# An encoder block on 8 cores: the last FFN product in one pass over 22 tiles, the attention accumulator kept by residue class, V and ones as column halves, x loads ahead of the constants

## What is computed

```
h = rms_norm(x, norm1_g)
proj = h @ w_in                                  # (2048, 9728)
# dilated: 3 groups, (window, dilation) = (128,1), (512,4), (2048,16), 8 heads of 64
#   per group: o_g = softmax(q k^T/8 - slope*dist, banded) v ; lse_g = m + log(denom)
#   merged over groups with softmax(lse) = sum_g numer_g / sum_g denom_g
x = x + (gates0*(y_dil@w_bd) + gates1*(y_ret@w_br) + gates2*(y_mem@w_bm)) @ w_out
u, gate = split(rms_norm(x, norm2_g) @ w_ffn_in)  # 2 x 2816 = 2 x 22 tiles of 128
x = x + (gelu(conv3(u) + b) * gate) @ w_ffn_out
```

## Time and profile before

| | us |
|---|---|
| median of 3 runs | 5742.73 (5291.3 to 5944.16) |
| profiled execution | 5273.2 |
| span of its slowest core (core 6) | 5271.6 |
| spans of the 8 cores | 5244.9 to 5271.6 |
| mean granted TensorE clock, by core | 0.988 to 0.991 |

### The profile page before, as it was taken

One profiled execution on the slowest core, in us unless ns is written; L12 is line 12 of the kernel. 1 busy time (PEld: TensorE's weight loads), 2 busy tenths in 40 slices (PEclk: granted clock), 3 DMA queues, 4 the chain that ended last, 5 costly groups with the idle time before them and its releaser, 6 DMA issues.

```text
span 5271.6 us, 85660 instructions; the slowest of 8 cores (5244.9 to 5271.6 us)
## 1 busy us (share of the span) xinstructions
PE 5008.7 (95%) x29335; PEld 2683.7 (51%) x29816; DVE 3290.3 (62%) x4398; ACT 2393.5 (45%) x4180; POOL 830.4 (16%) x874
## 2 busy tenths in 40 slices
PE   6999999999999999999999999999999999999999
PEld 3556644444455664444455666444445566544444
DVE  5566676656556667664656666766465666776544
ACT  5756543313376664331337665432134756633211
POOL 1322212111222110200112111020021211102000
PEclk9999999999999999999999999999999999999999
DMA  8368797766613335524350434542453143444344
GB/s 161 58 109 136 129 209 201 135 144 146 192 31 87 105 99 184 170 68 134 120 170 22 106 99 119 168 158 72 132 158 120 39 106 99 141 152 140 95 138 120
DMA packets 655785, 655.18 MB, mean 124 GB/s; under 512 B 368128, under 2 KB 411776, under 8 KB 655360
## 3 DMA queue, kind: packets, MB, share of 16 engines
q1 hardware_dynamic: 517712, 607.04, 39.6%
q0 software_dynamic: 137648, 42.64, 8.2%
HBM read 429.46 MB, written 212.34 MB: 122 GB/s over the span
## 4 chain that ended last, share of the span: by engine, by line
PE 85%; DMA 5%; DVE 4%; issue 3%; ACT 2%; POOL 1%; SPq 1%; DVEq 0%; ACTq 0%; POOLq 0%; another core or an unknown queue 0%
PE ps L833 40%; PE ps L1270 18%; PE ps L1610 8%; PE ps L1505 6%; PE ps L1536 3%; DMA tp<-out 3%; PE ps L1371 2%; PE ps L1033 2%; PE ps L1333 1%; DVE hT L908 1%; DMA arena<-x 1%; DMA wr<-w_in 1%; DVE arena L1381 1%; PE ps L1199 1%; PE ps L1201 1%
## 5 line engine op out<-in xcount | busy, mean ns | idle before, releaser
L833 PE MATMUL ps<-hT,wr 128*128 128x512 bf16 x9915 | 2271.7, 381 | 41.3 <-DMA wr<-w_in 7.1
L833 PEld LDWEIGHTS ps<-hT,wr 128*128 128x128 bf16 x10240 | 991.3, 98 | 1204.3 <-issue 67.2
L1270 PE MATMUL ps<-wr,hT 128*128 128x384 bf16 x6144 | 1055.8, 327 | 18.4 <-DVE arena L1381 9.5
L1270 PEld LDWEIGHTS ps<-wr,hT 128*128 128x128 bf16 x6144 | 716.0, 119 | 292.5 <-issue 32.4
L1610 PE MATMUL ps<-arena 128*128 128x512 bf16 x2760 | 617.0, 380 | 27.3 <-DVE tp L1613 23.9
L1576 ACT COPY arena<-ps 128x512 f32<-128x512 f32 x352 | 206.8, 587 | 689.5 <-PE ps L833 688.9
L1610 PEld LDWEIGHTS ps<-arena 128*128 128x128 bf16 x2816 | 273.3, 98 | 362.7 <-issue 41.7
L1585 DVE SCALAR_TENSOR_TENSOR tp<-arena,par,tp 128x1024 f32<-128x1024 f32 x352 | 450.8, 1303 | 9.5 <-DVE tp L1582 0.5
L1283 POOL TENSOR_TENSOR tp<-tp,gb 128x512 f32<-128x512 f32 x192 | 249.2, 1298 | 1302.1 <-ACT tp L1276 1302.1
L1276 ACT COPY tp<-ps 128x512 f32<-128x512 f32 x384 | 224.6, 585 | 417.2 <-PE ps L1270 415.6
L1286 DVE TENSOR_REDUCE sms<-tp 128x16 f32<-128x1024 bf16 x192 | 234.0, 1219 | 256.6 <-ACT tp L1277 253.5
(11 more groups left out here) (145 smaller groups left out, 5099.3 us busy)
## 6 DMA issues: line engine op xcount, KB each, us to landing
wr<-wsc SPq DMA_DIRECT2D x312, 256.0 KB, 3.4
gpre<-tp SPq DMA_DIRECT2D x256, 256.0 KB, 2.3
tp<-gpre SPq DMA_DIRECT2D x256, 256.0 KB, 5.3
tp<-out SPq DMA_DIRECT2D x256, 256.0 KB, 6.0
out<-tp SPq DMA_DIRECT2D x256, 256.0 KB, 4.8
arena<-x SPq DMA_DIRECT2D x64, 512.0 KB, 9.9
arena<-x SPq DMA_DIRECT2D x32, 1024.0 KB, 8.8
out<-arena SPq DMA_DIRECT2D x128, 256.0 KB, 6.3
```

What stands on the lines that cost most here:

```text
L833: ins = e.matmul(out, lhsT=w[:, kc, coff:coff + n], rhs=rhs_fn(kc), start=(kc == 0), stop=(kc == nk - 1))
L1270: ins = e.matmul(F(bk)[:, (j - j0) * 512:(j - j0) * 512 + 384], lhsT=hT[:, kc, t0:t0 + r * 127 + 1:r], rhs=w3()[:, kc, :], start=(kc == 0) ...
```

## The change

Five things change at once.

1. `F2_gen` runs once per sequence, over all 22 y tiles, after the whole of `F1_gen`; the y tiles get 22 places of their own. The loop is turned: output block oc outside, token block tt inside; the weights of one oc (22 blocks of 128 x 128) come as one tile of 3 slots in `wr` (new `wf2`; in the first sequence as two GpSimd DMAs of rows of 128 values). `A_gen` of the next sequence is woven with all of it and has two places for x in place of four.
2. In `pv`, V and ones are separate stationary operands of 64 columns: per piece four matmuls (V for heads 0 and 1, ones for heads 0 and 1) instead of two. Head hh writes partitions hh*64 to hh*64+63. Numerators lie in one bank, denominators in the other, and `fin_tile` works on all 128 partitions with one Ln, one Exp and one product. The memsets of L1257 go.
3. `acc` is kept by residue class mod 4 (`klass`), so dilation 4 writes without a stride, and dilation 1 reads its PSUM bank and `fin_tile` reads `acc` by class.
4. `consts()` is split: x of the first two blocks is loaded ahead of the constants; `gqk` and the distance table come after the first norm. In `O_gen` the first half of the first x block gets a place of its own, and the last block's norm is `direct`. The u projections of `F1_gen` lose their `gate`.
5. The scheduler's numbers: a window by stage (202 in dil, 144 in ret+mem, 145 in O, 96 in G and F) in place of 120, 0.13 in place of 0.1 for a change of mode while choosing, 260 in place of 280 bytes per ns for DMAs, and four tags moved in priority. Pool T gets a 16th slot.

```diff
+KN = {"wA": 202, "wR": 144, "wG": 96, "wO": 145, "wF": 96, "sw": 0.13, "slack": 0.06, "scan": 90, 
+      "late": {"mv": -22, "rq": -30, "rvar": 8, "gg": 8}}
...
-        o.pr = (o.i + late, o.i)
+        o.pr = (o.i + late + KN["late"].get(tag, 0), o.i)
+        o.win = KN[self.stage]
...
-                    if i > base + window:
+                    if i > base + ops[i].win:
...
                     if e == "tensor" and o.mode != mode:
-                        est += 0.1
+                        est += KN["sw"]
...
-                dma_t = st + o.dma / 280e3
+                dma_t = st + o.dma / 260e3
...
+    wsf = nc.dram_tensor("wsf", [8, 128, 2816], BF16, kind="Internal").ap()
...
-        NT, NT1, NW, NS = 15, 6, 9, 6
+        NT, NT1, NW, NS = 16, 6, 9, 6
...
+        def consts2():
             c4 = t4()
...
+            gq = t2()
+            P.op("sync", 0.06, lambda e: e.dma_start(out=F(gq)[:, 0:384], in_=gqk_d), writes=[gq], dma=196608)
...
-                xt = place((YB, YB + 8192, DB + 24576, DB + 32768)[t % 4], 8192, 2)
+                xt = place((YB, YB + 8192, DB + 24576, DB + 33280)[t % 4] if b == 0 else (DB + 24576, DB + 33280)[t % 2], 8192, 2)
...
-            u.dv = place(o + 8192, 6144, 16)
+            u.dv = place(o + 8192, 4096, 16)
...
+        def klass(r, sl):
+
+            return sl // 4 + sl % 4 * 4 if r == 16 else sl
...
-                P.op("gpsimd", 0.35, lambda e: e.memset(u.dvv[:, tt * 4:tt * 4 + 4, 64:128], 1.0), writes=[(u.dv, range(tt * 4, tt * 4 + 4))])
...
-                        t0 = cl + r * 128 * m
+                        t0 = klass(r, cl) + r * 128 * m
...
-                    P.op("scalar", c_act(256), lambda e: e.copy(out=u.dvv[:, ti0:ti0 + 2, :].rearrange("p j (a n) -> p j a n", a=3)[:, :, 0:3:2, :],
-                                                                in_=F(bk).rearrange("p (j n) -> p j n", j=2)[:, :, 256:384].rearrange("p j (a n) -> p j a n", a=2)),
+                    P.op("scalar", c_act(256), lambda e: e.copy(out=u.dvv[:, ti0:ti0 + 2, :], in_=F(bk).rearrange("p (j n) -> p j n", j=2)[:, :, 256:384]),
...
-                        for hh in range(2):
-                            ins = e.matmul(F(bk)[:, hh * 512 + oc:hh * 512 + oc + n], lhsT=u.dvv[:, ti, hh * 64:hh * 64 + 128],
-                                           rhs=H(p)[:, hh * 512 + pc:hh * 512 + pc + n], start=first_, stop=True, skip_group_check=True)
+                        for part in range(2):
+                            for hh in range(2):
+                                hp = slice(hh * 64, (hh + 1) * 64)
+                                ins = e.matmul(F(bk)[hp, part * 512 + oc:part * 512 + oc + n], lhsT=u.dvv[:, ti, hp] if part == 0 else ones[:, hp],
+                                               rhs=H(p)[:, hh * 512 + pc:hh * 512 + pc + n], start=first_, stop=True, skip_group_check=True)
                     return ins
...
-                    aslf = lambda: accv.rearrange("p h (i c) -> p h i c", c=r)[:, :, :, c0:c0 + 4]
-                    add(bk, aslf, lambda: F(bk).rearrange("p (h k i) -> p h i k", h=2, k=4), 1024, range(4))
+                    aslf = lambda: accv[:, :, c0 * 128:c0 * 128 + 512].rearrange("p h (i k) -> p h i k", k=4)
...
-                    aslf = lambda: accv[:, :, cl:cl + r * 511 + 1:r]
-                    add(bk, aslf, lambda: F(bk).rearrange("p (h i) -> p h i", h=2), 1024, range(4))
+                    aslf = lambda: accv[:, :, cl * 512:cl * 512 + 512]
...
-                    add(bk, lambda: accv[:, :, qb * 512:(qb + 1) * 512], lambda: F(bk).rearrange("p (h i) -> p h i", h=2), 1024, (qb,))
+                    add(bk, lambda: accv.rearrange("p h (c m) -> p h c m", c=4)[:, :, :, qb * 128:qb * 128 + 128], lambda: F(bk).rearrange("p (h i c) -> p h c i", h=2, c=4), 1024, range(qb, 16, 4))
...
-            sl = slice(qb * 512, (qb + 1) * 512)
             r = t2()
-            for hh in range(2):
-                hp, dp = slice(hh * 64, hh * 64 + 64), slice(64 - hh * 64, 128 - hh * 64)
-                P.op("scalar", c_act(512, False), lambda e: e.activation(out=F(r)[hp, :], in_=accv[dp, hh, sl], func=AF.Ln), reads=[(acc, qb)], writes=[r], phase=s.PE)
+            q4 = lambda i: accv[:, i, :].rearrange("p (c m) -> p c m", c=4)[:, :, qb * 128:qb * 128 + 128]
+            r4 = lambda: F(r).rearrange("p (c m) -> p c m", c=4)
+            P.op("scalar", c_act(512, False), lambda e: e.activation(out=r4(), in_=q4(1), func=AF.Ln), reads=[(acc, range(qb, 16, 4))], writes=[r], phase=s.PE)
             P.op("scalar", c_act(512, False), lambda e: e.activation(out=F(r), in_=F(r), func=AF.Exp, scale=-1.0), reads=[r], writes=[r], phase=s.PE)
-            for hh in range(2):
-                hp = slice(hh * 64, hh * 64 + 64)
-                P.op("vector", c_tt(512), lambda e: e.tensor_tensor(out=yv(s.ydil)[hp, c, sl], in0=accv[hp, hh, sl], in1=F(r)[hp, :], op=ALU.mult),
-                     c2=True, reads=[(acc, qb), r], writes=[(s.ydil, c * 4 + qb)])
+            P.op("vector", c_tt(512), lambda e: e.tensor_tensor(out=yv(s.ydil)[:, c, qb * 512:qb * 512 + 512].rearrange("p (m c) -> p c m", c=4), in0=q4(0), in1=r4(), op=ALU.mult),
...
-                xt = place(YB + (tt % 2) * 16384, 16384, 8)
+                base = YB + (tt % 2) * 16384
+                xt = [place(DB + 32768 if tt == 0 and hf == 0 else base + hf * 8192, 8192, 4) for hf in range(2)]
...
-                row_norm([(lambda k=k: AF_(xt, k * 512, 512), (xt, k)) for k in range(8)], 512, s.PN, P_N2G, tt * 512, pair_sq)
+                row_norm([(lambda k=k: AF_(xt[k // 4], k % 4 * 512, 512), (xt[k // 4], k % 4)) for k in range(8)], 512, s.PN, P_N2G, tt * 512, pair_sq, tt == 3)
...
-            s.u = [place(DB + (32768, 23552)[i], 8704, 4, ranges=lambda q: ((q * 2048, q * 2048 + 2056),)) for i in range(2)]
-            s.yslot = {j: (j if j < 11 else (11 + (j - 11) if j < 16 else j - 11)) for j in range(NJ)}
+            s.u = [place(DB + (33280, 24576)[i], 8704, 4, ranges=lambda q: ((q * 2048, q * 2048 + 2056),)) for i in range(2)]
...
-                    bk = proj("d", wu, tt, gate=s.PF, tag="fu")
+                    bk = proj("d", wu, tt, tag="fu")
...
+        def wf2(b, oc):
+            t = Tile(PW, 3, "w", nsub=2)
+            ap = lambda: wr[:, t.slot * 1024:t.slot * 1024 + 2816]
+            name = ("f2", oc)
+            if b == 0:
+                wkey[name] = Tile()
+                for h in range(2):
+                    P.op("gpsimd", 0.9, lambda e: e.dma_start(out=ap().rearrange("p (j n) -> p j n", j=NJ)[:, h * 11:h * 11 + 11, :],
+                                                              in_=w_f2[h * 1408:(h + 1) * 1408, oc * 128:(oc + 1) * 128].rearrange("(j p) n -> p j n", p=128)),
+                         writes=[(t, h)], dma=900000, tag="wc", ch=h)
+                if nseq > 1:
+                    P.op("sync", 0.06, lambda e: e.dma_start(out=wsf[oc], in_=ap()), reads=[t], writes=[wkey[name]], dma=720896, tag="ws")
+            else:
+                P.op("sync", 0.06, lambda e: e.dma_start(out=ap(), in_=wsf[oc]), reads=[wkey[name]], writes=[t], dma=720896, tag="wl")
+            return t
...
+        def F2_gen(s):
             b = s.b
...
+            for oc in range(8):
+                w = wf2(b, oc)
+                wv = lambda w=w: wr[:, w.slot * 1024:w.slot * 1024 + 2816].rearrange("p (j n) -> p j n", j=NJ)
+                for tt in range(4):
...
-                        for i, j in enumerate(js):
-                            ins = e.matmul(F(bk), lhsT=AH(ws[i])[:, oc * 128:(oc + 1) * 128], rhs=AH(s.y[j], tt * 512, 512), start=(i == 0), stop=(i == len(js) - 1))
+                        for j in range(NJ):
+                            ins = e.matmul(F(bk), lhsT=wv()[:, j, :], rhs=AH(s.y[j], tt * 512, 512), start=(j == 0), stop=(j == NJ - 1))
                         return ins
-                    P.op("tensor", len(js) * c_mm(512), f, reads=ws + [(s.y[j], tt) for j in js], writes=[bk], tag="f2")
...
-                    if oc % 2 == 1:
+                    if tt % 2 == 1:
...
-        for _ in range(4):
+        for k in range(4):
             run_all(islice(ag, 2))
+            if k == 0:
+                consts2()
             run_all(islice(rg0, 1))
+        consts3()
...
-            run_all(F1_gen(s, range(0, 11)))
-            weave((F2_gen(s, range(0, 11), 0), 16), (F1_gen(s, range(11, 16)), 5))
-            run_all(F1_gen(s, range(16, 22)))
+            P.stage = "wF"
+            run_all(F1_gen(s, range(NJ)))
...
-                weave((F2_gen(s, range(11, 22), 1), 16), (A_gen(cur), 8))
+                weave((F2_gen(s), 16), (A_gen(cur), 8))
+                P.stage = "wR"
...
-                run_all(F2_gen(s, range(11, 22), 1))
+                run_all(F2_gen(s))
```

64 lines of the change are left out of this document (35 added, 29 removed).

## The result

| | before | after |
|---|---|---|
| median, us | 5517.01 (4 runs) | 5314.58 (4 runs, 5223.15 to 5536.45) |
| profiled execution, us | 5273.2 | 5223.15 |
| mean span of a core, us | 5258 | 5210.1 |
| ratio, interval | | 0.9879, 0.985 to 0.9908 |

In some executions of every kernel one die (four of the eight cores) runs at a lower clock, which is why the medians lie so far above the profiled executions; such executions are left out of ratios, and the mean span is taken over the dies that kept their clock. The mean span is the finer measure: its standard error is 0.6 to 1.9 us for one kernel. The kernel before gave 5256 to 5260 in four groups of runs and 5252 in a fifth, so a difference of under about 5 us between kernels that were run in different groups is not told from none.

What follows compares the result with a forecast made beforehand. TensorE, busy 5008.7 of 5271.6 us, was taken as the bound; 46 + 8 - 38 - 14 - 20 - 4 - 10 - 4 = -36 took 5273 to 5237 us. Own range 5200 to 5280, over cases 5160 to 5310.

Steps and rivals of the forecast that it cites:

- halves on TensorE: P times V: mode changes and 64-column islands, paced from L995's paired matmuls, cost TensorE 46 us, from 25 to 55.
- (f): Strided adds, half-partition Ln and products, memsets and 128 adds leave VectorE, ScalarE and GpSimd; gain 10 us.
- (c): FFN product in one pass: fewer adds, less traffic of out, x loads spread out; gain 20 us, up to 34.
- (d): First sequence's FFN product: DMA casts of w_ffn_out in small packets; loss 8 us, from 0 to 35.
- (e): Program start: gqk and three parts of consts no longer before x; gain 4 us, from 0 to 10.
- scheduler's numbers: TensorE's order in ret+mem and dil: new numbers gain 4 us, bounds 0 and 106.
- (a): Passage from O to F: direct sum and projections ahead close TensorE's wait and low clock; gain 38 us.
- (b): O: waits for late x and the low clock behind them shrink by two thirds; gain 14 us.
- the lower bound: P times V, 64-column pieces: a pair costs 0.028 us, scaled from 128 columns; the upper end taken was 0.056.
- within 2%: Whole kernel: difference under about 2%, 105 us, not told from no change; chance 0.78.
- the 11 that the prediction named as its sign: dil stage in the profile after: longer by about 11 us per sequence, a quarter of 46, if right.
- the norm's company: Second FFN pass: next norm alongside costs 11 to 14 us beyond its own matmuls, some 36 in three sequences.

Runs made afterwards that it cites:

- e1: Changed kernel with P times V as two whole-array matmuls a piece, head 1's numerators and head 0's denominators left out; mean span 5162.6 us, ratio 0.9815.
- e13: Changed kernel without changes 2 and 3 (P times V, accumulator and division as before, 15 slots of T); mean span 5206.6 us, ratio 0.9892.
- e4: Kernel before with the one-pass FFN product and its places alone; mean span 5221.7 us against 5259.8, ratio 0.9919.
- e6: Changed kernel with all constants loaded ahead of the first x again; mean span 4.2 us above the changed kernel's 5210.1.
- e5: Changed kernel with the scheduler's numbers of the kernel before; mean span 5212.0 us, ratio 0.9901.
- e15: e1 with the division done in halves of 64 partitions by class, same parts left out; mean span 5221.6 us.
- e8: Changed kernel with the window of stage F at 120 and not 96; mean span 5216.2 us, ratio 0.9904.
- e11: Changed kernel, whole-array P times V with everything computed, first F1 weights loaded by O's window; mean span 5221.1 us against 5221.6 without that load.
- e14: e13 with the first tile of F1 loading its weights by the window of O; mean span 5210.8 us against 5206.6.

## Why the prediction was right and wrong

| term | forecast | measured | by |
|---|---|---|---|
| halves on TensorE | +46 | +47.5 | e1 |
| (f) work that leaves VectorE and ScalarE | -10 | -44 | e13 against the changed kernel, less e1 |
| (c) and (d) one pass, casts | -20 + 8 | -38 | e4 against before |
| (e) start | -4 | -4 | e6 |
| scheduler's numbers | -4 | -2 | e5 |
| (a) and (b), O and its passage to F | -52 | about -9 | the rest of e4 to e13 (-15) |
| sum | -36 | -48 | |

The measured terms add up to -49.5 and not to -48, since e4 and the whole change were set against slightly different means of the kernel before. The term of (a) and (b) is a remainder of four others and uncertain by some 5 us.

**The time.** 5237 was forecast for an execution like the profiled one, which came out at 5223. But the median that is reported is 5314.58, outside the range of 5160 to 5310. The step that failed for the time is the reference of the range: it was built from the mechanisms of the change around the level of 5273, although the median shown, 5742.73, said that such an execution is not the usual one. In the sum itself two steps failed, (f) and (a) with (b), in opposite directions.

**Right in place and size:** the halves, by the rows on L995; for 64 columns the lower bound was right (0.03 us a pair), not the upper that was taken. 0.03 us could have been read before, from the whole-array L1371 of 64 columns. The start and the numbers came as forecast, and within 2% was the likeliest class. The rule of the Trainium skill (TensorE: Matmul & The Clock Gate, LDWEIGHTS) that the forecast weighed, columns/1.2, 53 ns for 64 columns, would hold a pair at 53 ns; the pairs here follow each other every 30. Nor do they cost a quarter more than one whole-array matmul, which the prediction estimated from the 2.38x of the same page of the Trainium skill (Measured speedup vs the span model); that figure is for three tiles, which no run here has.

**(f) was too small by 34 us.** The step "they are under 70% busy; it shortens only the chains at the end of dil and the few waits in it" took VectorE's share of a stage for its slack. By e15, 24 us of VectorE and 10 of ScalarE work a sequence in dil, with the order that comes with them, cost 15 us a sequence. It is also why dil became only 5.5 us longer in the second to fourth sequence and not the 11 that the prediction named as its sign.

**(c) was worth its upper bound and more, (d) nothing.** The 34 us that the norm's company cost went entirely. The estimate of the DMA's work in the first sequence was near: 0.96 x 154.7 = 148 us there, beside what was loaded ahead; 4 of the 16 cast loads were issued ahead of the product, and there was no wait.

**(a) holds where it was placed but was too large, (b) hardly came: 43 us too much together.** The waits at the sum are gone (33.0 us before), and F of the changed kernel is 4.4 to 7.5 us a sequence shorter than in e4. (a) counted 15 us for the low clock by taking half of 30 us of stretches; TensorE was busy in 4.93 of 10.0 us and in 4.48 of 6.6, so half of the busy time, 9 us, was the price, and the rest is the wait itself, counted twice. Of (b), the wait for late x is still there: 11.4 us on the slowest core for 15.1, 11.6 for 13.4 in the mean of eight. And O became 8.6 us longer in that mean: some 6 are the two waits for weights, since the forecast followed TensorE's order at this place and not the loads on the queues of GpSimd and SyncE; another 5 are a projection more inside O in three sequences, moved and not added. Read by stage, F and O together are 18 us shorter than in e4 (there cores 4 to 7); that the remainder comes to 9 only means that part of it is lost in other stages, and where exactly stays open. e8, e11 and e14 show that removing the wait for weights does not bring it.

(f) with (c) and (d) was 60 us too small and (a) with (b) 43 us too large, so most of both errors cancelled, by luck. A forecast near the result is no sign that its terms were.

## What to carry to other kernels

Splitting a product to 64 output partitions cost TensorE only the way in and out here, about 0.1 us each, but count it per island, and ask what it saves the engines behind PSUM: an instruction on 64 partitions took as long as one on 128 (629 and 630 ns). A stride that is taken out of one operation goes into another; add up both. An engine at 65% of a stage still sets waits in it, so test by putting its work back alone, and a term that comes out as expected does not vouch for the others. Where the measure is a mean over cores, read the stages as a mean over cores too: the slowest core alone showed 15 us of loss in O where the eight show 9, and a wait of 8.3 us where they show 5.2.

## What was not expected of the hardware

VectorE's product to bf16 takes 820 ns for 64 x 512 in token order and 1376 to 1436 where it reads and writes by class, 1324 for 128 x 512; the additions 1220 without and 1630 in the mean with the strided ones. The clock's low stretches made some 28 of the 50 us between the slowest cores. In the kernel before, 15 of TensorE's 18 waits of 2 to 10 us past the start were followed by 3 to 10 us at half clock, in the changed kernel 4 of 8. The same 2.7 us wait in O (for L1540 before, for L1558 after) was followed by such a stretch in each of the last three sequences before (in the first a second wait of 3.0 us lay between) and in one of four after.
